# Strassen products for the dense gate and up of slices 3 to 6 in a two-layer decoder trunk

## What is computed

```python
h = h + gated_deltanet(rms_norm(h, a_norm), a_w_in, ...)       # linear attention, 8 heads, chunked
hn = rms_norm(h, ffn_norm[0])
h = h + (silu(hn @ w_gate) * (hn @ w_up)) @ w_down             # dense, 1024 -> 3584 -> 1024
k_sh, v_sh = shared_kv(h, ...)
h = h + sliding_window_attention(rms_norm(h, b_norm), k_sh, v_sh, ...)
h = h + moe_swiglu(rms_norm(h, ffn_norm[1]), ...)              # top 2 of 8 experts, same widths
```

## Time and profile before

| | |
|---|---|
| median of three runs | 1490.9 us |
| span of the profiled execution (first to last instruction) | 1489.1 us |
| TensorE busy | 1477.0 us, 99%, 7900 matmuls |
| VectorE busy | 1189.9 us, 80% |
| ScalarE busy | 947.9 us, 64% |
| GpSimd busy | 116.2 us, 8% |
| linear layer | 0 to about 190 us |
| dense halves 4 to 39 | 217 to 418 us |
| expert stage | from about 560 us |

### The profile page before, as it was taken

The page is one execution under the profiler, slowest core; times in us unless marked ns, Lnnn a source line. Parts: engine busy times, 40 slices in busy tenths (PEclk is TensorE's granted clock), DMA queues, the critical chain, the costliest instruction groups (busy, mean ns, idle before and its releaser), DMA issues.

```text
span 1489.1 us, 20171 instructions
## 1 busy us (share of the span) xinstructions
PE 1477.0 (99%) x7900; PEld 1234.6 (83%) x7900; DVE 1189.9 (80%) x1056; ACT 947.9 (64%) x852; POOL 116.2 (8%) x77
## 2 busy tenths in 40 slices
PE   9999999999999999999999999999999999999998
PEld 7999988888887788888888888888888888888886
DVE  5977775444478699889889889898898988988985
ACT  4554544434465676777677777677777677767773
POOL 0470110000013000000000000000000000000000
PEclk9999999999999999999999999999999999999999
DMA  6331885555414299999999999999999999999990
GB/s 227 114 115 58 307 320 181 173 209 183 169 58 156 99 396 393 396 383 393 397 382 394 393 369 386 381 371 381 383 380 372 389 380 363 391 383 359 395 362 30
DMA packets 186696, 445.60 MB, mean 299 GB/s; under 512 B 5399, under 2 KB 5680, under 8 KB 186635
## 3 DMA queue, kind: packets, MB, share of 16 engines
q1 hardware_dynamic: 182208, 430.12, 77.7%
q0 software_dynamic: 3936, 14.20, 3.3%
q10 hardware_dynamic: 490, 0.42, 0.1%
HBM read 437.89 MB, written 7.89 MB: 299 GB/s over the span
## 4 chain that ended last, share of the span: by engine, by line
PE 96%; DVE 2%; DMA 1%; ACT 0%; POOL 0%; issue 0%; SPq 0%; DVEq 0%; ACTq 0%
PE bank L1482 14%; PE bank L1484 14%; PE bank L1483 14%; PE bank L1467 7%; PE bank L1469 7%; PE bank L1468 7%; PE bank L698 4%; PE bank L1145 3%; PE bank L1144 3%; PE bank L1143 3%; PE bank L785 2%; PE bank L789 2%; PE bank L790 2%; PE bank L791 2%; PE bank L1132 1%; PE bank L1130 1%
## 5 line engine op out<-in xcount | busy, mean ns | idle before, releaser
L2625 DVE TENSOR_TENSOR ring_r<-ring,buf_r 128x2048 fp32r<-128x2048 f32 x336 | 751.2, 2284 | 28.0 <-ACT buf_r L1926 28.0
L1926 ACT ACTIVATE buf_r<-ring 128x2048 fp32r<-128x2048 f32 x336 | 629.4, 1914 | 52.5 <-PE bank L1469 43.3
L1482 PE MATMUL bank<-ring_r,buf_r 128*128 128x512 f32 x896 | 354.5, 396 | 0.3 <-DVE buf_r L2745 0.3
L1484 PE MATMUL bank<-buf_r,buf_r 128*128 128x512 f32 x896 | 349.6, 390 | 0.0
L1483 PE MATMUL bank<-buf_r,buf_r 128*128 128x512 f32 x896 | 349.0, 389 | 0.0
L1484 PEld LDWEIGHTS bank<-buf_r,buf_r 128*128 128x128 f32 x896 | 168.0, 188 | 36.0
L1482 PEld LDWEIGHTS bank<-ring_r,buf_r 128*128 128x128 f32 x896 | 168.4, 188 | 33.6 <-DVE buf_r L2745 0.4
L1483 PEld LDWEIGHTS bank<-buf_r,buf_r 128*128 128x128 f32 x896 | 168.5, 188 | 33.4
L1467 PE MATMUL bank<-ring_r,buf_r 128*128 128x512 f32 x440 | 172.8, 393 | 0.1
L1469 PE MATMUL bank<-buf_r,buf_r 128*128 128x512 f32 x440 | 171.5, 390 | 0.0
L1468 PE MATMUL bank<-buf_r,buf_r 128*128 128x512 f32 x440 | 171.2, 389 | 0.0
(11 more groups left out here) (378 smaller groups left out, 1867.1 us busy)
## 6 DMA issues: line engine op xcount, KB each, us to landing
ring<-in_moe_w_gate SPq DMA_DIRECT2D x56, 2048.0 KB, 10.0
ring<-in_moe_w_up SPq DMA_DIRECT2D x56, 2048.0 KB, 10.4
ring<-in_moe_w_down SPq DMA_DIRECT2D x56, 2048.0 KB, 10.4
ring<-in_a_w_in SPq DMA_DIRECT2D x8, 2048.0 KB, 8.5
ring<-in_dense_w_gate SPq DMA_DIRECT2D x7, 2048.0 KB, 7.8
ring<-in_dense_w_up SPq DMA_DIRECT2D x7, 2048.0 KB, 7.9
ring<-in_dense_w_down SPq DMA_DIRECT2D x7, 2048.0 KB, 8.0
ring<-in_a_w_out SPq DMA_DIRECT2D x2, 2048.0 KB, 10.9
```

What stands on the lines that cost most here:

```text
L1482: pe.matmul(o, xh, low[:, c], start=k == 0, stop=False)
L1484: ins = pe.matmul(o, xh, high[:, c], start=False, stop=k == KT - 1)
L1926: act.activation(HB[m % NHB], half_words(m, U_MOE), ACT.Copy).then_inc(m_wh, 1)
L2625: dve.tensor_tensor(half_low(m, U_MOE), half_words(m, U_MOE), HB[m % NHB], ALU.subtract).then_inc(m_wl, 1)
```

## The change

The gate (and the up) of two neighbouring slices is one product of 256 tokens by 1024 columns over a contraction of 1024. Cut in halves in all three directions it is 8 products of 128 by 512 by 512, each 12 matmuls. For slices 3 to 6, that is pairs 2 and 3 (`MIXED`), gate and up, these 4 "quads" are made of 7 products each. Slices 1 and 2 (pair 1, `PLAIN`) and slice 0 keep the plain form. The work is now in blocks of 1 MB, m = 0 to 53: a block of a plain weight or of a down weight still has 24 matmuls, a block of a quad 12, and each needs its own high and low part. Three of a quad's seven weight operands are sums of weight quarters that GpSimd's DMAs make in DRAM (`weight_sums`): six copies of 1 MB, four adding DMAs, two more adding DMAs for each pair; the fourth VectorE adds in the ring (`fourth_sum`). The four sums of the activations are made once (`mixed_rows`, `mixed_low`). The banks of a quad's output are put together by ScalarE, VectorE and GpSimd. The order of blocks is

The core of the diff (headings with @@ name the engine):

```diff
+def turns_after(p):
+    s = pair_at(p, "up")
+    if p in PLAIN:
+        return [s + 2, s + 3, s + 5, s + 6]
+    return [s + 5, s + 7, s + 8, s + 9]
...
@@ sync
+            def dense_loads():
+                for m in range(NB):
...
+                    if m < 4:
+                        sp.wait_ge(proj_mm, 16)
+                    elif m < 6:
+                        sp.wait_ge(vn_mm, 2)
+                    elif m < NB - 2 and block_before(m) < 0:
+                        sp.wait_ge(wo_mm, 4)
+                    elif m < NB - 2:
+                        sp.wait_ge(d_used, block_before(m) + 1)
...
+                    if BLOCKS[m][0] == "t":
+                        sp.wait_ge(sums_done, 16 * SUMS * (BLOCKS[m][1] // 2 + 1))
@@ gpsimd
+            def sums_start(n, picks):
+                for k in picks:
...
+                    pool.dma_start(sums(qd, r), quarter(quad_kind(qd), j, 0)).then_inc(sums_done, 16)
+            def sums_add(n, qd):
...
+                pool.wait_ge(sums_done, 16 * (SUMS * n + 6))
+                pool.dma_start(sums(qd, 2), quarter(kind, j, 1), accum_op=ALU.add, max_dma_last_dim=2048
+                               ).then_inc(sums_done, 16)
+                pool.dma_start(sums(qd, 0), quarter(kind, j, 0), accum_op=ALU.add, max_dma_last_dim=2048
+                               ).then_inc(sums_done, 16)
+            def sums_last(n):
+                pool.wait_ge(sums_done, 16 * (SUMS * n + 10))
+                for qd in (2 * n, 2 * n + 1):
+                    pool.dma_start(sums(qd, 1), sums(qd, 2), accum_op=ALU.add, max_dma_last_dim=2048
+                                   ).then_inc(sums_done, 16)
...
+            landed(pool, 1)
+            sums_start(0, [0, 1])
+            landed(pool, 2)
+            sums_start(0, [2])
...
             proj_low(6)
+            sums_start(0, [3, 4])
             for g in range(4):
                 level_mask(1, g)
             for g in range(4):
                 level_mask(2, g)
+            sums_start(0, [5])
             power(sm(248, UN), "half")
             for lv in range(3, NLEV - 1):
                 for g in range(4):
                     level_mask(lv, g)
+                if lv == 3:
+                    sums_add(0, 0)
                 if lv == 4:
...
+                    sums_add(0, 1)
+            sums_last(0)
+            landed(pool, 7)
+            pool.wait_ge(sums_done, 16 * SUMS)
+            sums_start(1, range(6))
             for t in range(TT):
                 power(sm(264 + t * HEADS, HEADS))
             power(sm(192, 1))
             pool.wait_ge(pow_out, powers[0])
-            pool.wait_ge(wo_mm, 3)
...
             power(sm(193, 1))
+            sums_add(1, 2)
+            sums_add(1, 3)
+            sums_last(1)
...
+            both_parts(0)
...
+            both_parts(1)
+            quad_hidden(MIXED[0])
+            both_parts(2)
+            both_parts(3)
+            quad_hidden(MIXED[1])
@@ tensor
+            def quad_products(qd):
+                m, p = quad_at(qd), quad_pair(qd)
+                if qd % 2:
+                    pe.wait_ge(sg_ready, silus_before(p) + 1)
+                elif p > 1:
+                    pe.wait_ge(pr_ready, hiddens_before(p) - (p - 1 in PLAIN))
+                product(m, A_BANK, rows_of(0, 0), start=True)
+                hidden_turns(m)
...
+                if p - 1 in PLAIN:
+                    pe.wait_ge(pr_ready, hiddens_before(p))
+                product(m + 1, B_BANK, mixed(1), start=True)
+                hidden_turns(m + 1)
+                product(m + 2, C_BANK, mixed(0), start=True)
+                hidden_turns(m + 2)
+                pe.wait_ge(first_out, 2 * qd + 1)
+                product(m + 3, A_BANK, rows_of(1, 0))
...
@@ scalar, loop over m
+                    act.wait_ge(d_used, high_free(m))
...
+                        if m == after + 5:
+                            hidden_high(2 * p - 1 + g // 2, g % 2)
+                    if m == s + 4:
+                        first_part(qd)
+                    if m == s + 6:
+                        fifth_part(qd)
...
+                if m < NB:
+                    dense_high(m)
@@ vector, loop over m
+                        if m == after + 5:
+                            hidden_low(2 * p - 1 + g // 2, g % 2)
+                    if m == s + 5:
+                        sixth_part(qd)
+                    if m == s + 7:
+                        if qd % 2 == 1:
+                            first_hidden(qd)
+                        last_piece(qd)
+                    if m == s + 9:
+                        side_pieces(qd)
+                    if m == s + 1:
+                        fourth_sum(qd)
+                for p in PLAIN:
+                    for i in range(4):
+                        if m == pair_at(p, "up") + 5 + i:
+                            plain_hidden(p, i // 2, i % 2)
+                if m < NB:
+                    dense_low(m)
```

More of the change, by code:

```diff
@@ L65, with quad_pair, quad_kind, dense_blocks @@
           ("o", 0, 0), ("o", 0, 1), ("o", 1, 0), ("o", 1, 1)]
+PAIRS = (NSL - 1) // 2
+PLAIN = [1]
+MIXED = [p for p in range(1, PAIRS + 1) if p not in PLAIN]
+QUADS = 2 * len(MIXED)
+TSUMS = 3
+SUMS = 12
+DSLOTS = RING[:6]
+def quad_pair(qd):
+    return MIXED[qd // 2]
+def quad_kind(qd):
+    return "up" if qd % 2 else "gate"
+def dense_blocks():
+    out = [("w", kind, 0, half) for kind in ("gate", "up") for half in range(2)]
+    for p in range(1, PAIRS + 1):
+        j = 2 * p - 1
+        for kind in ("gate", "up"):
+            if p in PLAIN:
+                out += [("w", kind, j + sl, half) for sl in range(2) for half in range(2)]
+            else:
+                qd = 2 * MIXED.index(p) + (kind == "up")
+                out += [("w", kind, j, 0), ("t", qd, 1), ("t", qd, 0), ("w", kind, j, 1), ("t", qd, 2),
+                        ("w", kind, j + 1, 1), ("t", qd, 3)]
+            if kind == "gate":
+                out += [("d", max(0, 2 * p - 3), half) for half in range(2)]
+            elif p > 1:
+                out += [("d", 2 * p - 2, half) for half in range(2)]
+    return out + [("d", j, half) for j in (NSL - 2, NSL - 1) for half in range(2)]
@@ new lines, with pair_at, quad_at, down_at @@
+BLOCKS = dense_blocks()
+NB = len(BLOCKS)
+SHORT = (NB // 2 - 1 - 5) % 6
+def pair_at(p, kind):
+    return BLOCKS.index(("w", kind, 2 * p - 1, 0))
+def quad_at(qd):
+    return pair_at(quad_pair(qd), quad_kind(qd))
+def down_at(j):
+    return BLOCKS.index(("d", j, 0))
+def turns_after(p):
+    s = pair_at(p, "up")
+    if p in PLAIN:
+        return [s + 2, s + 3, s + 5, s + 6]
+    return [s + 5, s + 7, s + 8, s + 9]
+def silus_before(p):
+    return 2 * TT + 4 * (p - 1)
+def hiddens_before(p):
+    return 2 * TT + sum(4 if i in PLAIN else 1 for i in range(1, p))
@@ new lines, in pool_part, with pool_hidden, block_loaded, block_place @@
+def pool_part(qd):
+    return qd + 1 + 3 * (qd // 2)
+def pool_hidden(p, i):
+    n = MIXED.index(p)
+    return 2 * (n + 1) + 3 * n + i
+def block_loaded(m):
+    return BLOCKS[m][0] != "t" or BLOCKS[m][2] < TSUMS
+def block_place(m):
+    n = m // 2
+    if n == NB // 2 - 1:
+        return 0, m % 2
+    return DSLOTS[n if n < SHORT else (n - SHORT) % 6], m % 2
+def block_uses(m):
+    s = block_place(m)[0]
+    return uses_before(s) + sum(block_place(i)[0] == s and block_loaded(i) for i in range(m - m % 2 + 2))
@@ L68, in slot_of, with block_before, high_place, high_free @@
+def block_before(m):
+    b = max((i for i in range(m) if block_place(i) == block_place(m)), default=-1)
+    return b if b < 0 or block_loaded(b) else b - b % 2 + 1
+def high_place(m):
+    return m % 4
+def high_free(m):
+    return m - 3
 def slot_of(n):
@@ L72, in slot_of, with uses_before @@
     return (n % FRONT if n < U_OUT else 5 * (n - U_OUT)) if n < U_FF else RING[(n - U_FF) % SLOTS]
+def uses_before(s):
+    return sum(slot_of(n) == s for n in range(U_KV))
 def uses(n):
-    return sum(slot_of(m) == slot_of(n) for m in range(n + 1))
+    s = slot_of(n)
+    blocks = sum(block_place(m)[0] == s and block_loaded(m) for m in range(NB)) if n >= U_KV else 0
+    return sum(slot_of(m) == s for m in range(n + 1)) + blocks
 def fill_bank(kind, n):
@@ L392, in static_units @@
             u += [("c", cols(a_w_out[0], n)) for n in range(2)]
-            w = {"gate": dense_w_gate[0], "up": dense_w_up[0], "down": dense_w_down[0]}
-            u += [("r", rows(w[k], j)) if k == "down" else ("c", cols(w[k], j)) for k, j in ffn_sequence()]
             u += [("c", cols(kv_w, 0))]
@@ new lines, in product @@
+                low, high = block_low(m), block_high(m)
+                for k in range(4):
+                    c = slice(k * FS, (k + 1) * FS)
+                    ah, al = of(k)
+                    pe.matmul(bk[bank][:, :], ah, low[:, c], start=start and k == 0, stop=False, skip_group_check=not start)
```

(13 more changed lines are left out.)

455 lines of the change are left out of this document (314 added, 141 removed).

## The result

The changed kernel takes **1509.0 us** (median; 1506.4 to 1509.7) against 1490.7 us beside it: 1.012 times as long, 95% interval 1.0106 to 1.0134. I had forecast 1488.0 us with 1497.0 as the upper end. The profiled execution took 1509.2 us; its span is 1507.3 us.

What follows compares the result with a forecast made beforehand. TensorE, busy 99% of the span, was taken as the bound. Terms -10.9 + 6.9 + 0.5 + 0.6 = -2.9 us gave a span of 1486.2 and a median of 1488.0 us, range 1481.5 to 1497.

Steps and rivals of the forecast that it cites:

- What goes, 10.9 us: Dense stage: four quads lose 12 matmuls each, 48 in all, saving 10.9 us of TensorE, the ceiling of the gain.
- The feed of a quad, 6.9 us in three stalls: Quads: TensorE stalls 2.7 us at block 15 and 2.1 each at the transposes behind blocks 16 and 32.
- Rivals 3 and 4: 3: stalls absent, 1481.1 us, chance 0.20; 4: VectorE falls behind in the quads, GpSimd holding its reads, 1503, chance 0.07.
- GpSimd beside VectorE, 0.5 us: Dense stage: ten new GpSimd instructions slow VectorE's low parts, 0.5 us, bounds 0 and 15.
- The linear layer, 0.6 us: Linear layer: sum transfers delay the loads of unit 4 and `a_w_out`, 0.6 us, bounds 0 and 5.3 + 1.8.
- Unit 4: Linear layer: two copies overlap its load at 232 instead of 400 GB/s, 1.8 us late, reserves leaving 0.1.
- `a_w_out`: Linear layer: second pair's copies moved by about 154 us, loads issued at 151.69; reserve 0.5 us, 1 us overlap costs 0.5.
- Rival 2: Linear layer: DRAM-to-DRAM copies at 3.4 us per MB last until 159, `a_w_out` lands 3 to 4 late: 1491, chance 0.13.
- Rival 1: Linear layer: GpSimd's power held behind the first pair's sums, TensorE stands 6 us at 10 us per MB: 1497.8, chance 0.15.
- three signs of being wrong: Forecast wrong if GpSimd's power came behind 156, low parts were much above 2.3 us, or the three stalls were missing.
- The sign that spoke: Linear layer: ScalarE's wait for `a_w_out` was to be up to 1 us longer.
- The dense loads, "5 to 9 us to spare": Dense stage: loads of m = 6 to 11 have 5 to 9 us to spare; 8 MB more find DMA half idle.

Runs made afterwards that it cites:

- e9_order_alone: Changed kernel without its 24 sum transfers, with ScalarE's and VectorE's instructions at blocks 15, 30, 31 and 48 placed earlier: 1483.6 us, 0.9948 of the kernel before.
- e1_no_sums: Changed kernel without its 24 sum transfers, sum blocks loaded as plain quarters of the weights: 1490.0 us, 0.9993 of the kernel before.
- e2_first_pair: Changed kernel without the second pair's 12 sum transfers, the first pair's 12 left in place: 1493.1 us.
- Experiment 2: Four runs on the changed kernel, second pair's 12 transfers from near 230 us; successively adding earlier first-pair copies and two instruction reorderings: 1511.3, 1508.1, 1507.3, 1506.9 us.
- e3_no_adding: Changed kernel with all 24 transfers, the 12 adding ones only copying: 1498.3 us.
- e4_order: Changed kernel with three groups of ScalarE's and VectorE's instructions one place earlier, at block 15 and behind blocks 16 and 32: 1502.5 us.
- e5_late_pair: Changed kernel with the second pair's 12 sum transfers started only when block 5 is used, near 230 us: 1511.3 us.
- e10_idle_hour: Changed kernel with earlier instruction places, two first-pair copies ahead of unit 3's low part, second pair's transfers from 187 us: 1501.7 us.
- e14_idle_hour_copies: `e10_idle_hour` with the second pair's six adding transfers only copying: 1488.4 us, 0.9983 of the kernel before.

## Why the prediction was wrong

- **What goes, 10.9 us**: held. In `e9_order_alone` the way from the transposes to the attention's first matmuls is 287.87 us against 296.52 before, 8.65 less with GpSimd's two stalls of 1 us left.
- **The feed of a quad, 6.9 us in three stalls**: the mechanism and the places were right. Block 15: 2.43 (forecast 2.7, its releaser not shown). Behind block 16: 1.46 to 1.80 (2.1). Behind block 32: 0.60, after 0.97 behind block 31, which I had called covered. Moved one place, they went, and the time by 6.4 us, restarts included. Rivals 3 and 4 fell.
- **GpSimd beside VectorE, 0.5 us**: 2 us, and elsewhere. Not the low parts as such were the loss, but the transposes in the up quads that wait for GpSimd's product (0.72 and 0.76 us, and some 0.25 for each restart, since the first matmuls behind an idle time last longer; an estimate from `e1_no_sums`: 10.9 us of matmuls less, 7.26 of idle time in six rows, and the way from the transposes to the attention 1.95 shorter, which leaves 1.7 / 6 = 0.28). I had written that the up quads show no gap.
- **The linear layer, 0.6 us: the step that failed.** It was 13.9. Unit 4: I took its load to keep 232 of 400 GB/s beside GpSimd's two copies, and so to be 1.8 us late. It got nothing while they ran. DMA by queue in 62 to 66 and in 66 to 72 us:

```profile
q0 software_dynamic: 357, 1.40, 104.2%
...
q1 hardware_dynamic: 812, 1.66, 86.4%
q0 software_dynamic: 49, 0.14, 9.7%
```

The load was issued at 61.95, and its first packets moved between 66 and 67 us; before the change they did so between 63 and 64, for an issue at 62.18. It landed after 13.5 us, not 7.9, which is three times the 1.8, and ScalarE waited 3.24 us for it (forecast 1.4). At `a_w_out`, issued at 154.56, the load got nothing until 158 us and then two fifths. DMA by queue in 155 to 158 and in 159 to 168 us:

```profile
q0 software_dynamic: 234, 0.92, 99.8%
...
q0 software_dynamic: 497, 1.90, 60.1%
q1 hardware_dynamic: 618, 1.27, 39.8%
```

The Trainium skill, DMA: Bandwidth & Descriptors, Queues, rings and completion order, says that the engines go round between the queues with work packet by packet; I had weighed that rule against the earlier trace rows and kept the row. The rows here follow neither: for 3 to 4 us copies issued earlier had the engines to themselves, and only behind that, at `a_w_out`, did the two queues share them. Why the load waits at first, no run here shows.

- `a_w_out`, the larger part of the same step: the copies ended near 168 us, not 154. Part is adding (5.6 us per MB, I had 5.0), more is copying (3.2, I had 2.4 from a row in which loads ran beside), the rest that GpSimd waited for unit 7, which landed 16.9 us after its issue, while the last adding transfers ran. I had seen the place, and had 0.5 us of reserve there behind 18 transfers, each kind priced from one row. Rival 2 had the mechanism and gave it 3 to 4 us; `e2_first_pair` against the changed kernel says 16 with what follows in the dense stage. Rival 1 fell: the power was at 153.85, shifted with everything else by 2.9. Of my three signs of being wrong (the power behind 156, low parts much above 2.3 us, no stalls) none came: they watched the other terms. The sign that spoke was ScalarE's wait for `a_w_out`, 9.5 us longer and not up to 1.
- **The dense loads, "5 to 9 us to spare"**: blocks 6 to 11 came late, and TensorE stood 2.10, 1.14 and 0.60 us. The half-idle DMA engines that I counted on are those of plain slices. Experiment 2 is the same error, made again.
- **The clock** stood in no term. Both idle times in the linear layer were followed by a stretch at 0.50: 2.5 us at the output product, up to 1.3 us at unit 4. In 290 to 310 us, around block 15's stall, it was 0.91 to 0.92, at most 1.7 us; with the same stall `e1_no_sums` kept 1.00.

The account: -10.9 of matmuls, 3.1 and 16.0 for the transfers of the two pairs, 6.4 for the order, 2.0 for GpSimd's products, make 16.6 of the 18.3 us. The other 1.7 us hang on the median of `e9_order_alone`, whose five runs spread from 1481.6 to 1485.1. Its profile, of the slowest, has 2.8 us outside the dense stage: the transposes begin at 188.64 us, 1.6 us later than before the change, behind an idle time of 1.91 us at 10.23 us for the load of `k_norm` and a clock of 0.66 in 10 to 15 us; and a clock of 0.50 in 514 to 516 us goes with another 1.4. Its two fastest runs, 1481.6, are what the other terms give: 1490.7 - 10.9 + 2.0 = 1481.8.

## What to carry to other kernels

Work moved to idle DMA engines has to be priced in DMA time, by the demand of the new schedule and not of the old one; an adding transfer took 5.6 us of all DMA engines per MB here, a copy 3.2. When a kernel works through an order written by hand, an instruction that frees a bank should stand ahead of the low part it has nothing to do with: halving the work between two such places turns a hidden wait into a stall. And a change that costs more than its gain at full size may gain at half: 24 matmuls and 12 transfers were faster, 48 and 24 in none of the orders tried here.

## What the runs showed of the hardware

- The clock's answer to one and the same idle time varied. At unit 4 TensorE stood 1.61 us in five of the profiles. In the changed kernel the clock fell at once (0.50 in 74 to 76 us), and the masks came 2.9 us late. In `e3_no_adding` and `e4_order` it held, TensorE stood again for 1.51 and 1.40 us at 78 us, and then it fell to 0.50, in 80 to 84 us: 5.9 and 5.7 us late. In `e5_late_pair` it held through both (1.61 and 1.36 us): 2.9 us. In `e2_first_pair` it was 0.50 from 74 to 78 us: 4.1 us late. So the 2.9 us came with the full clock as well as with the half one.
- A VectorE low part lasts 2.29 us alone and 2.95 to 3.00 where GpSimd's additions and products overlap it, a GpSimd product of 128 by 512 words 3.28 beside low parts and 1.26 in the masks (5.02 for four at 84.01 us): VectorE's and GpSimd's timelines of the changed kernel.

```profile
339.36 2.95 DVE L2745 TENSOR_TENSOR ring_r<-ring,buf_r 128x2048 fp32r<-128x2048 f32 x1 [0.35 <-ACT buf_r L2089]
...
350.13 3.00 DVE L2745 TENSOR_TENSOR ring_r<-ring,buf_r 128x2048 fp32r<-128x2048 f32 x1
...
343.58 3.28 POOL L876 TENSOR_TENSOR xbuf<-xbuf 128x512 f32<-128x512 f32 x1 [3.42 <-DVE xbuf L2851]
```

- Issuing four adding transfers took GpSimd 4.2 us (211.03 to 215.28 us in `e10_idle_hour`), the same four as copies 2.5 (212.77 to 215.30 in `e14_idle_hour_copies`).
- A load issued while GpSimd's copies were outstanding moved its first packets 4 to 5 us behind its issue (unit 4) and 3.4 to 4.4 (`a_w_out`); before the change both did within 2 us.
